# A two-layer hybrid mixer written as one order: projection tiles, SSD, attention and out projection interleaved, SSD exponents formed in PSUM

## The reference

```python
h -> [differential attention (4 heads) | windowed GQA with sink (4 heads) | bidirectional Mamba-2 SSD (8 heads)]
  -> one output projection
# differential attention: two softmaxes per head, a = p0 - lam * p1
s = jnp.einsum('bqhcd,bkhcd->bhcqk', q, k).astype(jnp.float32) * A_SCALE
p = jax.nn.softmax(s, axis=-1)
a = p[:, :, 0] - lam * p[:, :, 1]
```

## Time and profile before

| what | us |
|---|---|
| median of 3 runs | 2050.27 (2048.05 to 2052.09) |
| the profiled execution | 2050.99 |
| its span in the trace | 2049.2 |
| layer 0: projection after its first unit and SSD (462.6 to 652.6) | 190.0 |
| layer 0: attention (652.6 to 761.7) | 109.1 |
| layer 0: out projection (761.7 to 805.5) | 43.8 |
| layer 1: the same three stages, from 1589.5 | 168.2, 60.1, 23.3 |

### The profile page before, as it was taken

How to read it: one execution, slowest core, us unless ns; L and a number is a source line. 1 busy time by engine, 2 the same in 40 slices (tenths; PEclk the granted TensorE clock), 3 DMA queues, 4 the chain that set the end, 5 groups by cost and what they waited for, 6 DMA issues and landing times. The chain is left out here.

```text
span 2049.2 us, 25282 instructions
## 1 busy us (share of the span) xinstructions
PE 1802.8 (88%) x8940; PEld 1472.6 (72%) x8940; DVE 1465.1 (71%) x2465; ACT 716.3 (35%) x1043; POOL 94.0 (5%) x159
## 2 busy tenths in 40 slices
PE   0799999979956898999999979999997984788999
PEld 0588888857734456788888768888885773478999
DVE  7987878777577844978787767787856756746666
ACT  3422122244434544421222252222225433545342
POOL 0000000000022000000000000000000003000000
PEclk9999999989977988999999999999998986899999
DMA  8545444404233004454444414444421324134552
GB/s 316 189 166 183 150 157 164 164 21 136 104 81 64 1 22 184 165 184 145 162 164 162 166 62 144 167 144 181 143 84 43 128 103 69 14 124 144 184 184 103
DMA packets 39917, 269.97 MB, mean 132 GB/s; under 512 B 5104, under 2 KB 6448, under 8 KB 9136
## 3 DMA queue, kind: packets, MB, share of 16 engines
q1 hardware_dynamic: 25776, 183.28, 24.9%
q0 software_dynamic: 14080, 85.89, 13.0%
HBM read 262.99 MB, written 5.37 MB: 131 GB/s over the span
## 5 line engine op out<-in xcount | busy, mean ns | idle before, releaser
L1253 PE MATMUL ps<-h_hi,w_hi 128*128 128x512 f32 (+1 forms) x1872 | 690.0, 369 | 70.5 <-DVE h_lo L832 70.5
L1254 PE MATMUL ps<-h_lo,w_hi 128*128 128x512 f32 (+1 forms) x1872 | 684.4, 366 | 0.0
L1255 PE MATMUL ps<-h_hi,w_lo 128*128 128x512 f32 (+1 forms) x1872 | 683.9, 365 | 0.0
L1253 PEld LDWEIGHTS ps<-h_hi,w_hi 128*128 128x128 f32 x1872 | 357.2, 191 | 139.3 <-issue 69.1
L763 DVE TENSOR_TENSOR w_lo<-raw,w_hi 128x2048 fp32r<-128x2048 f32 (+1 forms) x162 | 366.4, 2262 | 97.4 <-ACT w_hi L470 97.3
L861 DVE SCALAR_TENSOR_TENSOR x_res<-ps,abg,x_res 128x256 f32<-128x256 f32 x640 | 272.0, 477 | 204.8 <-PE ps L1255 186.2
L470 ACT ACTIVATE w_hi<-raw 128x2048 fp32r<-128x2048 f32 (+1 forms) x162 | 306.3, 1891 | 279.2 <-PE ps L1255 275.3
L1254 PEld LDWEIGHTS ps<-h_lo,w_hi 128*128 128x128 f32 x1872 | 356.9, 191 | 57.7 <-issue 1.2
L1255 PEld LDWEIGHTS ps<-h_hi,w_lo 128*128 128x128 f32 x1872 | 356.4, 190 | 57.6
L780 DVE CUSTOM_DVE_ANT_0 mod_prod<-mod_raw,cb 128x1024 f32<-128x1024 f32 x288 | 338.3, 1218 | 14.8 <-DMA mod_raw<-mod_in 13.3
L1253 PE MATMUL ps<-a_hi,w_hi 128*128 128x512 f32 (+1 forms) x704 | 258.1, 367 | 15.6 <-DVE a_lo L855 13.4
(11 more groups left out here) (162 smaller groups left out, 1266.5 us busy)
## 6 DMA issues: line engine op xcount, KB each, us to landing
raw<-ffn_in SPq DMA_DIRECT2D x132, 1024.0 KB, 4.9
mod_raw<-mod_in POOLq DMA_DIRECT2D x72, 1024.0 KB, 5.1
raw<-proj_in SPq DMA_DIRECT2D x20, 1024.0 KB, 5.6
raw<-out_w_in SPq DMA_DIRECT2D x8, 1024.0 KB, 4.8
x_spill<-x_res SPq DMA_DIRECT2D x2, 2048.0 KB, 7.3
eo<-decay_rows POOLq DMA_DIRECT2D x8, 512.0 KB, 5.5
x_res<-x_spill SPq DMA_DIRECT2D x2, 2048.0 KB, 8.9
cb<-c_in SPq DMA_DIRECT2D x2, 1024.0 KB, 9.5
```

The lines of the kernel that those rows point to most:

```text
L1253: pe.matmul(dst, w_hi[:, slot, wsl], hi, start=first, stop=False)
L1254: pe.matmul(dst, w_hi[:, slot, wsl], lo, start=False, stop=False)
L1255: return pe.matmul(dst, w_lo[:, slot, wsl], hi, start=False, stop=last)
```

## The change

Nothing of the result changes. The list `STEPS` and the three stages behind it are replaced by one order of steps, made by `steps(layer)`, which every engine walks, each taking the steps that it has a part in.

- **Projection tiles one by one.** `PROJECT` lists tiles ("T", g) of one bank each, in banks 0 and 1, in place of units of two. The dt tile comes first, its matmuls in turn with those of the first convolution tile (`first_tiles`). The four parts of the decay rows ("R", 0) to ("R", 3) follow at once on ACT and DVE, before the convolutions. Key and query means have bank 2, rotations and value transposes bank 3.
- **SSD inside the projection.** ("x"), ("s"), ("r") are the states. ("hx", i), 16 of them, form an exponent on PE in bank 4 or 5: a mask (`ident_r` by `drop_r`), the query's decays (a picked row of `e_rows`, 512 or 256 wide), and the key's decays, one matmul of 128 columns for each chunk. ACT exponentiates from the bank into `m_t`, a ring of 6, and ("hm", i) on DVE multiplies with `cbt`. ("hc", h), 8 of them, spread the decay of C over the partitions with two fp32 matmuls into bank 7, and DVE multiplies. ("hy", t) are the products as before, in bank 6, and ("hg", t) the gate. The DMAs of `eo`, the DVE subtractions (64 of 128x128 in layer 0) and POOL's `cexp` are gone.
- **Attention with work beside it.** For each item i the order is scores(i), weights(i-1), maximum(i), values(i-2), then what `BESIDE` lists for i, then transposes(i-1), exponential(i), copy(i-1). The scales of the scores lie in the norm's gains, and the maximum is negated by the reduction itself, which saves a small DVE instruction per item. `BESIDE` holds the last two gate tiles (19 and 20), the gates' silu, the split of the last unit, the group norms, and parts of the out projection of tiles m = 0 to 3: "Os" (4 of 8 contraction blocks, the SSD's) and "Oa" (2, the A items'). "Ob" (the last 2) and "Of" (all 8, of tiles 4 to 7) follow after attention. Transposes have one bank (6) and values one bank (7), in place of two each.
- **Loads.** The mixer's loads alternate over two buffers, and each waits for the split of the unit two before it. The third buffer belongs to the feed-forward blocks alone, and their first loads wait for all splits before them. `x_res` is fetched back once the last SSD product is done.

```diff
+        PROJECT = [("T0", 0), ("E", 0), ("R", 0), ("E", 1), ("R", 1), ("S", 0),
+                   ("T", 2), ("E", 2), ("cv", 0), ("R", 2), ("S", 1),
...
+                   ("T", 12), ("s", 1), ("b", 3), ("E", 12), ("hx", 0), ("hx", 1), ("c", 2), ("r", 1), ("x", 2), ("S", 6),
+                   ("T", 13), ("v", 0), ("E", 13), ("s", 2), ("hx", 2), ("hx", 3), ("c", 3), ("hm", 0), ("hm", 1), ("r", 2),
+                   ("T", 14), ("v", 1), ("E", 14), ("hc", 0), ("hc", 1), ("hm", 2), ("hm", 3), ("hx", 4), ("hx", 5), ("S", 7),
+                   ("T", 15), ("hy", 0), ("b", 4), ("E", 15), ("hm", 4), ("hm", 5), ("hg", 0), ("hx", 6), ("hx", 7), ("c", 4),
+                   ("T", 16), ("b", 5), ("E", 16), ("hc", 2), ("hc", 3), ("hm", 6), ("hm", 7), ("hx", 8), ("hx", 9), ("c", 5), ("S", 8),
+                   ("T", 17), ("hy", 1), ("v", 2), ("b", 6), ("hm", 8), ("hm", 9), ("hg", 1), ("hx", 10), ("hx", 11), ("c", 6),
...
+        BESIDE = {0: {0: [("Ta", 19)], 1: [("Tb", 19), ("E", 19)], 2: [("Ta", 20)], 3: [("Tb", 20), ("E", 20)], 4: [("zs", 0), ("S", 10)],
+                      5: [("g", 0), ("g", 1)], 6: [("g", 2), ("g", 3), ("sq", 0), ("me", 0)], 7: [("sq", 1), ("me", 1), ("ro", 0)],
...
+        def steps(layer):
+
+            n = len(att_items(layer))
+            order = PROJECT + [("hy", 3), ("hg", 3), ("E", 17), ("E", 18)]
+            for i in range(n + 2):
+                front = [("sc", i), ("wt", i - 1), ("mx", i), ("pv", i - 2)]
+                back = [("tr", i - 1), ("ex", i), ("ev", i - 1)]
+                order = (order + [s for s in front if 0 <= s[1] < n] + BESIDE[layer].get(i, [])
+                         + [s for s in back if 0 <= s[1] < n])
+            return order
 
         ORDER = [[2, 3, 0, 1], [3, 2, 1, 0]]
...
                 for m in range(MIX_UNITS):
-                    u = base + m
+                    sp.wait_ge(lo_ready, base - 2 if m == 0 else base - 1 if m == 1 else base + m - 1)
...
+                    if m == PROJ_UNITS + 1:
+
+                        sp.wait_ge(hd_mm, 4 * (layer + 1))
+                        sp.wait_ge(spilled, 16 * (layer + 1))
+                        sp.dma_start(x_res[:, :, :].rearrange("p k t -> p (k t)"), spill).then_inc(x_back, 16)
...
-                def decay_rows_of(h):
-
...
-                    both = rows_dram[layer, 0].rearrange("(d h) t -> h d t", d=2)[h]
-                    pool.dma_start(eo[:, h % 2, 0:2, 0:nt], both[:, 0:nt].partition_broadcast(P)).then_inc(eo_in[h % 2], 16)
-                    for d in range(2):
-                        pool.dma_start(eo[64 * d:64 * d + 64, h % 2, 2, 0:nt],
-                                       rows_dram[layer, 1, 8 * d + h, 0:nt].partition_broadcast(64)).then_inc(eo_in[h % 2], 16)
-
-                def scaled_c(h):
-
-                    pool.wait_ge(eo_in[h % 2], rows_in(layer, h))
-                    if h >= 4:
-                        pool.wait_ge(hd_mm, 4 * layer + h // 2 - 1)
-                    pool.tensor_tensor(cexp[:, h % 4, 0:nt], c_two[:, h // 4, 0:nt], eo[:, h % 2, 2, 0:nt], ALU.mult).then_inc(cexp_done, 1)
...
-                for r in range(DECAYS):
-                    h, d = r // 2, r % 2
-                    act.wait_ge(d_done, DECAYS * layer + r + 1)
-                    for c in range(nt // P):
-                        seg = dd[:, h % 4, d, c * P:(c + 1) * P]
-                        x = act.activation(seg, seg, ACT.Exp, bias=dcol[:, c, 32 + 8 * d + h:33 + 8 * d + h])
-                    x.then_inc(ex_done, 1)
-                attention(layer)
...
+                    elif kind == "hx":
+                        act.wait_ge(x_mm, DECAYS * layer + j + 1)
+                        if j >= RING:
+                            act.wait_ge(hd_mm, 4 * layer + (j - RING) // 4 + 1)
+                        act.activation(m_t[:, j % RING, 0:nt], ps[:, 4 + j % 2, 0:nt], ACT.Exp).then_inc(ex_done, 1)
...
-                def exponents(r):
-                    h, d = r // 2, r % 2
-                    if d == 0:
-                        dve.wait_ge(eo_in[h % 2], rows_in(layer, h))
-                        if h >= 4:
-                            dve.wait_ge(hd_mm, 4 * layer + h // 2 - 1)
-                    for c in range(nt // P):
-                        x = ts(dd[:, h % 4, d, c * P:(c + 1) * P], eo[:, h % 2, d, c * P:(c + 1) * P],
-                               dcol[:, c, 8 * d + h:8 * d + h + 1], 0.0, ALU.subtract, ALU.min)
-                    x.then_inc(d_done, 1)
...
+                if what == "hm":
+                    dve.wait_ge(ex_done, DECAYS * layer + i + 1)
+                    m = m_t[:, i % RING, 0:nt]
+                    tt(m, m, cbt[:, i // 8, 0:nt // P, :].rearrange("p c t -> p (c t)"), ALU.mult).then_inc(mt_done, 1)
+                elif what == "hc":
+                    dve.wait_ge(ce_mm, HEADS * layer + i + 1)
+                    if i == 0:
+                        dve.wait_ge(c_two_in, 64 * (layer + 1))
+                    if i >= 2:
+                        dve.wait_ge(hd_mm, 4 * layer + i // 2)
+                    tt(cexp[:, i % 2, 0:nt], c_two[:, i // 4, 0:nt], ps[:, 7, 0:nt], ALU.mult).then_inc(cexp_done, 1)
...
-                    dve.tensor_reduce(sm[:, 0:nc_], ps[:, 2 * (e % 2):2 * (e % 2) + nc_, 0:nk], AX_X, ALU.max).then_inc(mx_done, 1)
                     if kind == "A":
-                        dve.wait_ge(mx_done, mxb[0] + 1)
+                        dve.tensor_reduce(sm[:, 2:4], ps[:, bank:bank + 2, 0:nk], AX_X, ALU.max, negate=True).then_inc(nmx_done, 1)
+                    else:
                         mxb[0] += 1
-                        ts(sm[:, 2:4], sm[:, 0:2], -A_SCALE, None, ALU.mult).then_inc(nmx_done, 1)
+                        dve.tensor_reduce(sm[:, 1:2], ps[:, bank, 0:nk], AX_X, ALU.max, negate=True).then_inc(mx_done, 1)
+                        dve.wait_ge(mx_done, mxb[0])
+                        tt(sm[:, 2:3], sm[:, 1:2], lam[:, 88 + h:89 + h], ALU.min).then_inc(nmx_done, 1)
+                    return
+
+                p0, p1 = e_att[:, e % 2, 0, 0:nk], e_att[:, e % 2, 1, 0:nk]
...
-                for e in range(len(items) + 1):
-                    if e < len(items):
-                        maxima(e)
-                    if e >= 1:
-                        weights(e - 1)
-                    norms(e)
...
+                if what == "hx":
+                    h, d = i // 2, i % 2
+                    r = 8 * d + h
+                    pick = sel_r[:, r:r + 1].to_broadcast([P, P])
+                    if i == 0:
+                        pe.wait_ge(row_dve, ROW_STEPS * (layer + 1))
+                        pe.wait_ge(xt_evac, 8 * (layer + 1))
+                        pe.wait_ge(const_r, 2)
+                    if i >= 2:
+                        pe.wait_ge(ex_done, DECAYS * layer + i - 1)
+                    bank = 4 + i % 2
+                    pe.matmul(ps[:, bank, 0:nt].rearrange("p (c t) -> p c t", c=nct), ident_r[:, :],
+                              drop_r[:, d, :].unsqueeze(1).to_broadcast([P, nct, P]), start=True, stop=False)
+                    pe.matmul(ps[:, bank, 0:nt], pick, e_rows[:, 0:nt], start=False, stop=False)
+                    for c in range(nct):
+                        last = pe.matmul(ps[:, bank, c * P:(c + 1) * P], g_rows[:, c * P:(c + 1) * P], pick,
+                                         start=False, stop=c == nct - 1)
+                    last.then_inc(x_mm, 1)
+                elif what == "hc":
+                    pe.wait_ge(cexp_done, HEADS * layer + i)
+                    if i == 0:
+                        pe.wait_ge(st_done, 6 * (layer + 1))
+                    for d in range(2):
+                        last = pe.matmul(ps[64 * d:64 * d + 64, 7, 0:nt], sel_r[:, 8 * d + i:8 * d + i + 1].bitcast(F32).to_broadcast([P, 64]),
+                                         x_rows[:, 0:nt].bitcast(F32), start=True, stop=True)
+                    last.then_inc(ce_mm, 1)
```

1164 lines of the change are left out of this document (601 added, 563 removed), and 28 rows, old and new, of tables (BESIDE, PROJECT, STEPS).

## The result

The changed kernel takes 2072.5 us (median of 11 runs, 2069.2 to 2076.8), the kernel before 2055.6 in the same comparison (2045.5 to 2069.2). The ratio is 1.008, interval 1.0053 to 1.0108: the change makes the kernel slower by 0.8%. I had forecast 2042. The profiled execution took 2072.51 us with a span of 2070.5, against 2050.99 and 2049.2 before, so the two traces differ by 21.3 us.

What follows compares the result with a forecast made beforehand. PE, busy 88%, was taken as the bound, losing time to waits and clock in the mixers. Projection -7.1 and -17.9, attention -3.3 and +14.3, loads +2, clock +4: -8.0 on 2050.99, 2043; median 2042, the case's range 2024 to 2060.

Steps and rivals of the forecast that it cites:

- The new length of the projection: Projection and SSD: 172 us against 190 in layer 0, 144.6 against 168.2 in layer 1; real gains 7.1 and 17.9.
- the first tiles: Start of each mixer's projection: given no term in the sum, so taken as unchanged.
- The stall at the fifth tile: Projection, layer 0: PE stops about 6 us at tile 5, since DVE's first convolution starts some 11 us later.
- The chain of weights, maximum and exponential: Attention A items: the three become one dependent chain, 4.45 us per 512-key item, about 3.2 per 256-key one.
- My sum for attention with its moved work: Attention plus moved tiles and out projection parts: 132 us against 135.1 in layer 0, 88.4 against 74.1 in layer 1.
- rival B: Attention A parts fall to half clock and PE sets the pitch: 2070 us, range 2060 to 2090, chance 0.23.
- from which it decides: A items: at half clock PE's work per item exceeds the 4.45 us chain, so PE sets the pitch.
- The 5.3 us: A items: PE's work per item at half clock, twice the 2.66 us at full clock.
- Rival A: Mixers: PE becomes dense, half the stalls and attention loss go: about 2000 us, range 1985 to 2030, chance 0.27.
- the walk's 60 us of stalls: Projection and SSD: PE stalls from walking the new order, 26.5 us in layer 0, 34 in layer 1.
- Rival C: Projection: 128-column matmuls cost as much as 512-column ones, spreads 0.94 twice, 21 us more on PE: 2052, chance 0.05.
- the 4 put for the clock: Attention A parts: 4 us over both layers for a lower PE clock, with ends 0 and 25.

Runs made afterwards that it cites:

- control: The changed kernel run once more, unedited, as the yardstick of the other experiments: 2071.7 us, ratio 1.0068.
- early-split run: Changed kernel with DVE's split of the mixer's unit 1 put ahead of the eight normalized tiles: 2066.4 us, ratio 1.0047.
- the fill: Changed kernel with useless PE matmuls in the idle stretches behind the silu block, 24 in layer 0 and 20 in layer 1: 2073.4 us.

## Why the prediction was wrong

The forecast said 2042 with most of the chance on faster, and the kernel became slower, within the range. By its own steps, against the traces (-8 forecast, +21.5 measured):

- **"The new length of the projection", from the first tiles on.** Right in kind. An exponent takes 0.95 us, as I had taken it: two stand between 558.12 and 560.02 here (start, length; L1469 opens an exponent, L1433 comes behind the second).

```profile
558.12 0.50 PE L1469 MATMUL ps<-drop_r,ident_r 128*128 128x512 f32 x1
...
559.08 0.45 PE L1469 MATMUL ps<-drop_r,ident_r 128*128 128x512 f32 x1
...
560.02 0.70 PE L1433 MATMUL ps<-qk,const 128*128 128x256 f32 x2
```

  A spread takes 1.0 (568.47 to 569.48), taken as 0.9. The stall at the fifth tile was 2.8 us and not 6, the idle sum 20.8 and 23.9 us and not 26.5 and 34. But PE was busy for 155.6 and 122.4 us where I had added up 145.5 and 110.6: part of this work ran at half clock (0.94 and 0.93). The stretches came out at 176.4 and 146.3, where I had 172 and 144.6: 6 us missing. The control's trace, at half clock for 13 us and not 25, is 4.4 us shorter in layer 0, so most of them are the clock. The longest wait was not the 6 us at the fifth tile but 3.8, for a spread.
- **The step that failed: the first tiles, which I left out of the sum as unchanged.** I put nothing for them. In fact the second split stands behind six tiles on DVE, and the code shows that the first matmuls wait for both units: 17.6 us from the mean to the first matmul in place of 7.2. 10.4 us per layer are lost, 3 per layer come back since the tiles then run dense: +14.8, enough to turn the forecast of -8 into a loss. The early-split run shows that the start is this wait (7.2 again). It also shows that not all of it is there to win: put right, it gave 5.3 us alone and 9.9 beside the fill, since my projection would then have come out longer.
- **The A items.** The chain of weights, maximum and exponential was the right mechanism: 4.45 forecast, 4.37 measured, and the order of these two steps in the kernel before makes it alone, for 19 us. A parts 75.6 and 45.0 against 72 and 46. My sum for attention with its moved work was a gain of 3.3 in layer 0 and a loss of 14.3 in layer 1, counted from the first maximum; measured are losses of 3.9 (139.0 against 135.1) and 16.3 (90.4 against 74.1). Of the 9 us between, 5.7 are the B parts, 62.5 and 45.2 in place of 60 and 42, and 2.6 the A parts. The silu block (6.6 us, with 5.75 of idleness in layer 0) stands in the A part of layer 0, but no run shows its price: moving it by itself made the kernel slower.
- **What I had not seen** is that the same step also shortened the lookahead of the scores from two items to one. As long as the weights stand first it doesn't show in free items (4.37 us apart, 4.58 in the kernel before with two items and the weights first). But the obvious repair (the maximum first) was a loss of 21 us with it. Two items of lookahead with the maximum first were still a loss of 16, so the short lookahead is not the whole reason; the weights first with two items of lookahead were not run in the woven kernel.
- **The out projection and the ends.** 30.2 us in place of 27.3 in layer 0, at a mean clock of 0.90 behind the last items' idle time. At the end of layer 1, 8.45 us pass to the mean, 4.2 before: the splits of the feed-forward's first units stand ahead of the last updates on DVE, and wait for a load that is issued only when the last mixer split is done. I had put 1 us. The split waits, and so do the updates behind it:

```profile
1856.52 2.29 DVE L818 TENSOR_TENSOR w_lo<-raw,w_hi 128x2048 fp32r<-128x2048 f32 x1 [4.93 <-ACT w_hi L494]
1858.72 0.87 DVE L922 SCALAR_TENSOR_TENSOR x_res<-ps,abg,x_res 128x256 f32<-128x256 f32 x2
```

```profile
1866.05 1.22 PE L1309 MATMUL ps<-n_acc,const 128*128 128x256 f32 x2 [8.45 <-DVE n_acc L886]
```

- **The rivals.** The measured time is rival B's, 2070, but as far as the runs go its mechanism did not decide it, so that the number fits it is luck. The clock did fall to 0.50 in the A parts, for 21 and 17 us; still, taking 7 and 6 us of that away gained nothing (2073.4 against 2071.7). The point "from which it decides" was wrong: free items keep their pitch at half clock, here and in the kernel before with the weights first. The 5.3 us were too high as well: in layer 1 of that kernel the longest step between exponentials of 512 keys at a clock of 0.50 is 4.78 us, with PE busy throughout (1770.29 to 1775.07), so half clock brings PE about level with the chain. The Trainium skill, TensorE: Matmul & The Clock Gate, section "A second HAM failure mode: psum-queue depth-cycling", says that short idle times between groups of matmuls can make the clock swing between its levels; the trace agrees (1.00, 0.50, 1.00, 0.50, 1.00 in the A part of layer 0, the second fall behind idle times of at most 1.07 us). Whether that costs anything is decided here by who sets the pace: it did in the B items of layer 1 (53.5 us against 44.8) and in layer 1's A items with two items of lookahead (47.4 against 44.7, 39.4 against 36.5).
- Rival A (the stalls vanish): 16 of the walk's 60 us of stalls did, but the chain of the A items stayed, and with it the loss. Rival C fell with the 0.95 of an exponent and the 1.0 of a spread.
- **Slips in the sums.** The parts given for attention in layer 1 (35.6, 10, 28, 8.4 and 5) make 87.0 and not 88.4, a loss of 12.9 and not 14.3; in layer 0 the gain is 135.1 - 132 = 3.1, not 3.3; and 24 matmuls at 0.121 are 2.9 and not 2.8. Put right, the forecast moves by less than 2 us.

Summed, from -8 to +21.5: +14.8 start, +6.1 projection, +8.9 attention and out projection beyond the 4 put for the clock, +1.4 ends, -1.9 elsewhere, 29.3 of 29.5.

## What to carry to other kernels

When steps are reordered so that one needs a second input at once, look where that input is made on the other engine: its old place was chosen when nobody waited for it. In a pipeline over items, count for each engine how many items its steps lie apart; order within an item and lookahead between items act on each other, and putting one right by itself can lose more than it gains (the maximum first alone: 21 us). Work put beside a chain of dependent steps is free only for the engine that has slack there: two parts of the out projection beside the A items of layer 0 were; behind a block of silus with two table loads and a split, on the engine of the exponentials, PE stood idle for 5.75 us.

## What the runs showed of the hardware

- The same program's projection stage has different lengths from one execution to the next. From the mixer's first matmul to the first scores of layer 0, the traces of kernels with equal code there gave 185.1 us three times, about 188 twice and 189.3 to 189.8 five times; their time at half clock was 13 us in the shortest, 19 in the middle ones and 22 to 25 in the longest. Layer 1 gave 158.7 to 160.1 (at half clock for 23 to 29 us), and 165 in two (39 us). A difference of a few us between two traces is nothing there.
- Once the granted clock was at 0.50 it stayed there for stretches of full work: in the version with the exponentials first, from 668 to 692 us in layer 0, though PE was busy for all of 684 to 688 in it. In the kernel before with the weights first it was at 0.50 for 19.2 us in which PE was busy throughout:

```profile
694.00:713.20 19.20, 19.20 (x68) 10.88 (x66) 12.21 (x31) 8.35 (x25) 0.00 (x0) 0.50 0.00 0
```

  Matmuls without use, issued into the idle time, held it up while they ran, at no cost where PE had been waiting anyway; in the A part of layer 0 it fell all the same later (at 677.3 in the fill's own run), behind idle times of at most 1.71 us.
- In the kernel before, 54 us from the mixer's first matmul to the first scores of layer 0 and 74 of layer 1 were at half clock; in the woven one 25 and 23 (control: 13 and 29).
